# Two tiles of constants padded to whole multiples of 128 bytes in a two-block transformer kernel

## The chip, the cores and the metric

The kernel runs on one NeuronCore of a Trainium2 chip. The metric is the device time of one launch in microseconds. Three runs of the kernel before gave 2766.96, 2767.59 and 2768.25 us, so the median is 2767.59 us.

## The reference

All arithmetic is in float32, for one sequence of 512 tokens of width 1024. Two blocks follow each other. Cut to what matters:

```python
def reference(x, mem, ...):
    x = first_block(x, mem, ...)
    return second_block(x, ...)

def first_block(...):
    x = x + rms_norm(hybrid_mixer(rms_norm(x)), post)            # sparse attention beside an mLSTM
    x = x + rms_norm(memory_cross_attention(rms_norm(x), rms_norm(mem)), post)
    x = x + rms_norm(swiglu_ffn(rms_norm(x), w_gate_up, w_down), post)

def second_block(...):                                            # two layers
    # per layer: h += 0.5 ffn1(h); h += conformer_conv(h) (layer 0)
    #            or stick_breaking_attention(h) with shared keys (layer 1); h += 0.5 ffn2(h)
    return rms_norm(h, final_norm)
```

Five of the stages are SwiGLU feed-forward layers: 1024 columns to twice 2816, and 2816 back to 1024. They hold most of the multiplications.

## The kernel before

Activations lie transposed, with the features over the 128 partitions and the 512 tokens along each partition. A dense stage multiplies weight blocks of 128 by 128, which are the stationary operand (they are loaded with LDWEIGHTS, written PEld in the profile), with 256 tokens at a time of the activations, which are the moving operand of the MATMUL. Each float32 product is made of three in the type fp32r: high part of the weight times high part of the activation, low times high, and high times low. So every tile of weights and every tile of activations stands in memory twice, as a high and as a low part.

SyncE streams the weights into `w_raw`, a ring of four slots of 4,096 bytes per partition. ScalarE writes the high parts (`w_hi`), VectorE the low parts (`w_lo`, and `w_below` in the feed-forward stages). The order of the work is written out by hand in one block per engine, and semaphores hold the engines together.

- Dense stages (`unit`, line 646) multiply `w_hi` and `w_lo` with `h_hi`, `h_lo`, or with `m_*` and `o_*` in the memory and output stages. Where they are the second half of a feed-forward layer ("down"), the activations lie in `t_hl`, `a_below` and, for the last chunks, in `wx`.
- The gate and up products of the feed-forward layers (`product`, line 812) are done in pairs by a scheme with seven block products in place of eight. Sums of weight blocks are needed for it. They lie in `wx` (the sums S1 and S2 and the low part of A22), in `w_lo` and in `w_hi`. The moving operand is always in `t_hl`. In these stages `wx` holds weights and is a stationary operand, in the down stages it holds activations and is a moving one.
- `cmp_unit` (line 965) is the one place where the roles are turned: the small tile `g_hl` is stationary and 256 columns of `w_hi` or `w_lo` move past it.
- The sums over features for the norms are plain float32 products with one column of `cst` as the moving operand (lines 1406 and 1413: `cv`, then `sq`, are stationary).

The tiles are placed in the order in which they are declared (from line 215 on), each at the next multiple of 32 bytes, and tiles of different phases overlay each other. `vec` is 472 floats wide (1,888 bytes) and `cst` 1,301 floats (5,204 bytes). The built program has these starts in bytes of a partition:

| tile | start | past a multiple of 128 | behind `cst` |
|---|---|---|---|
| `w_raw`, `w_below` | 16,512 | 0 | no |
| `w_lo` | 32,896 | 0 | no |
| `w_hi` | 49,280 | 0 | no |
| `x` | 65,664 | 0 | no |
| `vec` | 82,048 | 0 | |
| `cst` | 83,936 | 96 | |
| `rB`, `sq`, `acc`, `t0`, `t1` | 89,152 and on | 64 | yes |
| `h_hi`, `h_lo` | 101,696, 118,080 | 64 | yes |
| `t_hl`, `o_hi`, `yb_x`, `qT` | 134,464 | 64 | yes |
| `m_hi`, `m_lo`, `qkv`, `u_conv`, `a_below` | 160,064 and on | 64 | yes |
| `cv`, `diag_w`, `c_acc`, `c_product` | 184,576 and on | 0 | yes |
| `toep`, `decay`, `n_p`, `g_hl` | 180,192 and on | 96, `g_hl` 32 | yes |
| `wx` | 216,384 | 64 | yes |

Slots, blocks and chunks inside the tiles are multiples of 512 bytes, so a product's operands keep the residue of their tile. `u_conv` is 17,344 bytes wide, which is 135.5 times 128. That is why the tiles behind it have another residue than the others.

The diff touches the declaration of `vec` and `cst` and the two transfers that fill them.

Of the kernel before, what the change touches and what calls it, by code (L numbers as in the profile page):

```python
# [140 lines left out]
def starts(sizes):  # L141

    found, at = {}, 0
    for name, size, *_ in sizes:
        found[name], at = at, at + size
    return found, at
# [13 lines left out]
VEC, NVEC = starts(VECTORS)  # L160
CST, NCST = starts(CONSTS)


def rounds(eng, n, peel=0):

    for i in range(min(peel, n)):
        yield i
    if n > peel:
        with eng.Fori(peel, n) as i:
            yield i  # L170


class Steps:
# [14 lines left out]
    def loop(self, n, per, peel=0):  # L188
        first = self.base + self.n
        for i in rounds(self.eng, n, peel):  # L190
            self.base, self.n = first + i * per, 0
            yield i
            assert self.n == per, (self.n, per)
        self.base, self.n = first + n * per, 0


def block_program(nc, t, out):
# [4 lines left out]
    with ctx:  # L202
        def held(stack):
            return lambda name, width, dt=f32: stack.enter_context(nc.sbuf_tensor(name, [P, width], dt))

        sb = held(ctx)

        def sem(name):
            return ctx.enter_context(nc.semaphore(name))
# [6 lines left out]
            w_raw, s_raw = held(h)("w_raw", RING * UNIT), held(h)("s_raw", RING * UNIT)  # L216
        w_below, w_lo, w_hi = sb("w_below", RING * UNIT, f32r), sb("w_lo", RING * UNIT, f32r), sb("w_hi", RING * UNIT, f32r)
        x = sb("x", KC * S)
        vec, cst = sb("vec", NVEC), sb("cst", NCST)
        rB = sb("rB", S)  # L220
        sq, acc = sb("sq", 2 * S), sb("acc", S)
        t0, t1 = sb("t0", S), sb("t1", S)
# [79 lines left out]
        vec_in, cst_in, mem_in = sem("vec_in"), sem("cst_in"), sem("mem_in")  # L302
# [136 lines left out]
        def centred(eng, c):  # L439
# [3 lines left out]
            else:  # L443
                eng.wait_ge(c_conv, c + 1)

        stage_blocks = {n: b for n, _, b in STAGES}
        def in_bank(i):
            return bank[(i + 1) % 3]
# [82 lines left out]
        def _(sp):  # L531
            def load_x(i):
                sp.dma_start(cut(x, i, 2 * S), t["x"][:, 2 * i:2 * i + 2].rearrange("p c n -> p (c n)")).then_inc(x_in[i], 16)

            load_x(0)
            sp.dma_start(vec[:], t["vectors"]).then_inc(vec_in, 16)

            def load(slot, src, q):

                u = 4 * q + slot  # L540
                if not (isinstance(q, int) and u < RING):
                    sp.wait_ge(w_lo_made, u - 3)
                width = src.shape[-1]
                sp.dma_start(w_raw[:, slot * UNIT:slot * UNIT + width], src).then_inc(raw_in[slot], 16)
# [4 lines left out]
            def stage(name, w):  # L549
                w = flat(w)  # L550
                q0 = U0[name] // RING
                for it in rounds(sp, w.shape[0] // RING):
                    for j in range(RING):
                        load(j, w[bass.ds(RING * it + j, 1)].rearrange("u p n -> (u p) n"), q0 + it)
# [24 lines left out]
            def stage_down(name, w, pairs):  # L579
                w = flat(w)  # L580
                q0 = U0[name] // RING
                g_end = PAIR0[pairs] + NPAIRS[pairs]
                for it in rounds(sp, KC // 4, peel=1):
                    for j in range(12):
                        if isinstance(it, int) and it == 0 and j < RING:
                            sp.wait_ge(pair_used, 6 * (g_end - 2 + j // 2) + 4 + j % 2)
                        k0, kn = DN_KS[j % 3]
                        src = w[bass.ds(4 * it + j // 3, 1), :, k0 * P:(k0 + kn) * P].rearrange("u p n -> (u p) n")
                        load(j % RING, src, q0 + 3 * it + j // RING)

            w_in, w_cmp, w_gates = flat(t["w_in"]), flat(t["cmp_w1"]), t["w_gates"].rearrange("p k n -> p (k n)")
            for r, (kind, n) in enumerate(IN_ORDER):
                load(r % RING, {"block": w_in, "cmp": w_cmp}[kind][n] if kind != "gates" else w_gates[:, n * 4 * P:(n + 1) * 4 * P],
                     r // RING)
                if r == 0:
                    load_x(1)
                if r == 1:
                    load_x(2)
                    load_x(3)
                if r == 2:  # L600
                    sp.dma_start(cst[:], t["consts"]).then_inc(cst_in, 16)

            stage("out", t["w_out"])
            stage("xkv", t["w_xkv"])
# [37 lines left out]
        def _(pe):  # L642
# [751 lines left out]
            def ln_sums(i):  # L1394
                m = LN_ORDER[i]
                _, at, n = PIECES[m]
                if i == 0:
                    pe.wait_ge(ln_s_made, 1)
                if m == KC:

                    pe.wait_ge(ln_parts, 2)
                    pe.wait_ge(ln_var_made, 1)

                centred(pe, m)
                for b in range(at // P, (at + n) // P):
                    last = nc.tensor.matmul(bank[7][:, b:b + 1], conv_out(m)[:, b * P - at:(b + 1) * P - at], const("one"),
                                            start=i == 0 and b == 0, stop=i >= KC - 1, skip_group_check=True)
                if i >= KC - 1:
                    last.then_inc(stat_done, 1)
                pe.wait_ge(c_sq, i + 1)  # L1410
                for b in range(at // P, (at + n) // P):
                    sq_at = (i % 2) * S + b * P - at
                    last = nc.tensor.matmul(bank[6][:, b:b + 1], sq[:, sq_at:sq_at + P], const("one"), start=i == 0 and b == 0,
                                            stop=i >= KC - 1, skip_group_check=True)
                last.then_inc(stat_done if i >= KC - 1 else c_sums, 1)
# [193 lines left out]
        def _(act):  # L1609
# [434 lines left out]
            def products(m, i0, i1):  # L2044
                c, _, width = PIECES[m]
                p = SHARES[m][0]
                for i in range(i0, i1):
                    n = PRODUCT0[m] + i
                    if i == 0:
                        act.wait_ge(c_glu, m + 1)  # L2050
                    if n >= 4:
                        act.wait_ge(c_product_used, n - 3)
                    nc.scalar.activation(cut(c_product, n % 4)[:, 0:width], conv_tap(m, p + i), ACT.Identity, scale=col("w_dw", c * TAPS + p + i),
                                         bias=col("b_dw", c) if i == 0 else const("zero")).then_inc(c_product_made, 1)
# [1358 lines left out]
```

## Time and profile before

| | |
|---|---|
| runs, median (lowest to highest) | 2767.59 us (2766.96 to 2768.25) |
| the profiled execution, its own time | 2768.85 us |
| its span, first to last instruction | 2766.9 us |
| mean granted TensorE clock | 0.991 of full speed |
| instructions | 53,376, of them 22,432 MATMUL |
| HBM traffic | 253.29 MB read, 8.42 MB written |

The profiled execution took 1.26 us more than the median of the runs, which is 0.05%. PE is TensorE at matmuls, PEld its weight loads, DVE is VectorE, ACT is ScalarE, POOL is GpSimd. A matmul's duration in the profile reaches from its first column to the end of its pipeline, and consecutive ones overlap. What it costs the engine is the distance from one start to the next. In a view by stretches of time, "(x885)" is the number of instructions that touch the stretch, so the two or three that began before it are counted too.

### The profile page before, as it was taken

Reading aid. Unit: us, or ns where it says so; the run is one execution under the profiler, and the core shown is the slowest. Engines: PE = TensorE matmul, PEld = TensorE weight load, DVE = VectorE, ACT = ScalarE, POOL = GpSimd, SP = SyncE. Lnnn points to the kernel's source line nnn. Section 1 sums busy time; section 2 is a strip of 40 time slices with the busy share of each in tenths; the row PEclk is TensorE's granted clock in tenths of the full one; section 3 lists DMA queues with packets and bytes.
Section 4 is the critical chain, followed back from the end, with each engine's and each line's share of the span. In section 5 each row is a group of like instructions: output and inputs, shape, how many; then the busy total and the mean of one; then the engine's idle time right before and its main releaser. Section 6 shows DMA issues by size and latency. Waiting matters only on the chain.

```text
span 2766.9 us, 53376 instructions
## 1 busy us (share of the span) xinstructions
PE 2709.6 (98%) x22432; PEld 2586.7 (93%) x22432; DVE 1830.9 (66%) x2650; ACT 1296.3 (47%) x2052; POOL 239.4 (9%) x212
## 2 busy tenths in 40 slices
PE   8999999999999999999999999999999999999998
PEld 8977998999999999997799999999999987999998
DVE  6786753888626888348868884338886367587743
ACT  4465524545524455246754553215554246445531
POOL 0010201000000000018710000000000000100000
PEclk9999999999999999999899999999999999999999
DMA  6320431223332233322122333342333332223332
GB/s 214 110 67 17 129 101 47 92 84 102 119 102 77 85 107 113 97 90 62 39 65 89 106 105 108 92 155 84 105 106 118 94 126 88 62 87 106 99 111 73
DMA packets 76266, 265.10 MB, mean 96 GB/s; under 512 B 8388, under 2 KB 10564, under 8 KB 75776
## 3 DMA queue, kind: packets, MB, share of 16 engines
q1 hardware_dynamic: 69408, 248.93, 29.0%
q10 hardware_dynamic: 5632, 8.39, 0.8%
q0 software_dynamic: 992, 4.42, 0.5%
q8 instruction: 176, 2.88, 0.4%
q14 instruction: 58, 0.48, 0.1%
HBM read 253.29 MB, written 8.42 MB: 95 GB/s over the span
## 4 chain that ended last, share of the span: by engine, by line
PE 89%; DVE 4%; ACT 3%; issue 2%; DMA 1%; POOL 1%; SPq 0%; DVEq 0%; POOLq 0%; ACTq 0%
PE bank L646 48%; PE bank L812 30%; PE bank L701 2%; DMA w_raw<-in_w_gu 1%; DVE bank L3013 1%; PE bank L766 1%; DVE w_lo L2268 1%; POOL c_acc L3286 1%; PE bank L1463 1%; PE bank L1542 1%; PE bank L1381 1%; PE bank L1562 1%; PE bank L990 1%; PE bank L1117 1%; PE bank L1331 0%
## 5 line engine op out<-in xcount | busy, mean ns | idle before, releaser
L2268 DVE TENSOR_TENSOR w_lo<-w_raw,w_hi 128x1024 fp32r<-128x1024 f32 (+1 forms) x296 | 358.4, 1214 | 351.3 <-ACT w_hi L1621 184.7
L812 PE MATMUL bank<-t_hl,w_hi 128*128 128x256 f32 x2752 | 534.3, 282 | 17.4 <-issue 13.9
L812 PEld LDWEIGHTS bank<-t_hl,w_hi 128*128 128x128 f32 x2752 | 443.1, 189 | 19.8 <-issue 19.3
L1621 ACT ACTIVATE w_hi<-w_raw 128x1024 fp32r<-128x1024 f32 (+1 forms) x296 | 298.3, 1024 | 236.8 <-PE bank L646 156.9
L646 PE MATMUL bank<-h_hi,w_hi 128*128 128x256 f32 x1936 | 388.4, 282 | 11.4 <-DVE w_lo L2268 11.4
L646 PE MATMUL bank<-t_hl,w_hi 128*128 128x256 f32 x2128 | 386.9, 281 | 0.0
L646 PE MATMUL bank<-h_lo,w_hi 128*128 128x256 f32 x1936 | 380.0, 278 | 0.0
L646 PE MATMUL bank<-h_hi,w_lo 128*128 128x256 f32 x1936 | 379.9, 278 | 0.0
L812 PE MATMUL bank<-t_hl,wx 128*128 128x256 f32 x1720 | 360.3, 281 | 0.0
L646 PE MATMUL bank<-t_hl,w_lo 128*128 128x256 f32 x1672 | 333.8, 281 | 0.0
L812 PE MATMUL bank<-t_hl,w_lo 128*128 128x256 f32 x1720 | 331.6, 283 | 0.0
L646 PEld LDWEIGHTS bank<-h_hi,w_hi 128*128 128x128 f32 x1936 | 294.6, 189 | 20.1 <-DVE w_lo L2268 11.0
L646 PEld LDWEIGHTS bank<-t_hl,w_hi 128*128 128x128 f32 x2128 | 309.0, 188 | 0.0
L646 PEld LDWEIGHTS bank<-h_lo,w_hi 128*128 128x128 f32 x1936 | 293.9, 189 | 0.0
L646 PEld LDWEIGHTS bank<-h_hi,w_lo 128*128 128x128 f32 x1936 | 293.7, 189 | 0.0
L812 PE MATMUL bank<-t_hl,w_below 128*128 128x256 f32 x1032 | 290.9, 282 | 0.0
L812 PEld LDWEIGHTS bank<-t_hl,wx 128*128 128x128 f32 x1720 | 287.5, 189 | 0.0
L812 PEld LDWEIGHTS bank<-t_hl,w_lo 128*128 128x128 f32 x1720 | 261.5, 192 | 0.0
L646 PEld LDWEIGHTS bank<-t_hl,w_lo 128*128 128x128 f32 x1672 | 256.5, 190 | 0.0
L3238 POOL TENSOR_TENSOR acc<-acc,sq 128x512 f32<-128x512 f32 (+1 forms) x63 | 81.5, 1294 | 1648.5 <-ACT sq L1627 1646.8
L812 PEld LDWEIGHTS bank<-t_hl,w_below 128*128 128x128 f32 x1032 | 198.8, 193 | 0.0
L646 PE MATMUL bank<-a_below,w_hi 128*128 128x256 f32 x912 | 181.7, 281 | 0.0
(394 smaller groups left out, 4619.1 us busy)
## 6 DMA issues: line engine op xcount, KB each, us to landing
w_raw<-in_w_gu SPq DMA_DIRECT2D x220, 512.0 KB, 3.6
w_raw<-in_w_dn SPq DMA_DIRECT2D x80, 512.0 KB, 3.6
w_raw<-in_w_dn SPq DMA_DIRECT2D x40, 384.0 KB, 3.2
w_raw<-in_w_pw SPq DMA_DIRECT2D x24, 512.0 KB, 3.6
w_raw<-in_w_in SPq DMA_DIRECT2D x22, 512.0 KB, 4.5
w_raw<-in_w_xkv SPq DMA_DIRECT2D x16, 512.0 KB, 3.6
w_raw<-in_w_kv SPq DMA_DIRECT2D x16, 512.0 KB, 3.6
stick_qkv<-t ACTq DMA_DIRECT2D x24, 256.0 KB, 2.0
```

The lines of the kernel that those rows point to most:

```text
L646: last = nc.tensor.matmul(dst[:, c:c + HALF], w, o[:, at + c:at + c + HALF], start=start and c == 0, stop=stop, skip_group_check=True)
L701: last = nc.tensor.matmul(dst[:, 0:HALF], w[:, at:at + P], src, start=start and i == 0 and m == 0, stop=stop and i == len(ks) - 1 and m == 2)
L766: last = nc.tensor.matmul(dst, w[:, at:at + P], half_of(o, k, half), start=half == 0 and k == 0 and m == 0, stop=k == KC - 1 and m == 2, s ...
L812: last = nc.tensor.matmul(pair_bank(s, which), w[:, i * P:(i + 1) * P], o, start=start and i == 0 and m == 0, stop=stop and i == 3 and m = ...
L990: nc.tensor.matmul(bank[2 * (s % 2) + half][:, 0:nsa_n(s)], qT[rs, c * S + qb * P:c * S + (qb + 1) * P], (kS, kW)[br - 1][rs, 0:nsa_n(s)], ...
L1117: last = nc.tensor.transpose(bank[4 + half][:, k * P:(k + 1) * P], nsa_p(s, half, S)[:, k * P:(k + 1) * P], ident)
L1381: last = nc.tensor.matmul(tap_bank(m), w, conv_tap(m, k), start=k == 0, stop=k == n - 1)
L1463: last = nc.tensor.matmul(bank[PW2_BANKS[0][j]][:, tokens(half)], w[:, at:at + P], half_of(o, k, half), start=half == 0 and k == 0 and m = ...
L1542: last = nc.tensor.matmul(z[half][:, 0:n], qT_[rs, qb * P:(qb + 1) * P], kT[rs, S - n:S], start=False, stop=True, skip_group_check=True)
L1621: nc.scalar.activation(w_hi[:, at:at + n], w_raw[:, at:at + n], ACT.Copy).then_inc(w_hi_made, 1)
L2268: V.tensor_tensor(w_lo[:, at:at + n], w_raw[:, at:at + n], w_hi[:, at:at + n].bitcast(f32), sub).then_inc(w_lo_made, 1)
L3238: G.tensor_tensor(acc[:, 0:n], acc[:, 0:n], sq[:, (c % 2) * S:(c % 2) * S + n], add).then_inc(summed, 1)
```

## The change

`vec` is declared with 480 columns in place of 472, and `cst` with 1,312 in place of 1,301. That is 32 and 44 bytes, 76 in all. `vec` then ends at a multiple of 128 bytes, `cst` begins and ends at one, and what lies behind it begins 64 bytes later than before (12 of the 76 bytes were lost before to the multiple of 32). The transfers fill the same 472 and 1,301 columns as before. Nothing else is edited: the instructions, their order, their sizes and the semaphores are the same.

```diff
+def lines(width):
+
+    return -(-width // 32) * 32
+
...
-        vec, cst = sb("vec", NVEC), sb("cst", NCST)
+        vec, cst = sb("vec", lines(NVEC)), sb("cst", lines(NCST))
...
-            sp.dma_start(vec[:], t["vectors"]).then_inc(vec_in, 16)
+            sp.dma_start(vec[:, 0:NVEC], t["vectors"]).then_inc(vec_in, 16)
...
-                    sp.dma_start(cst[:], t["consts"]).then_inc(cst_in, 16)
+                    sp.dma_start(cst[:, 0:NCST], t["consts"]).then_inc(cst_in, 16)
```

After the edit, by the same order of placing, `h_*`, `t_hl`, `o_*`, `m_*`, `a_below`, `wx`, `sq` and `acc` begin at multiples of 128 bytes. `cv`, `diag_w`, `c_acc` and `c_product` begin 64 bytes past one, `g_hl` 96 past one. The weight tiles `w_below`, `w_lo`, `w_hi` lie ahead of `vec` and do not move.

## Rows read from the trace of the kernel before

**Rows 1.** The page, part 1: busy time, share of the span, instructions

```profile
PE 2709.6 (98%) x22432; PEld 2586.7 (93%) x22432; DVE 1830.9 (66%) x2650; ACT 1296.3 (47%) x2052; POOL 239.4 (9%) x212
```

**Rows 2.** The page, part 4: the chain that ended last

```profile
PE 89%; DVE 4%; ACT 3%; issue 2%; DMA 1%; POOL 1%; SPq 0%; DVEq 0%; POOLq 0%; ACTq 0%
PE bank L646 48%; PE bank L812 30%; PE bank L701 2%; DMA w_raw<-in_w_gu 1%; DVE bank L3013 1%; PE bank L766 1%; DVE w_lo L2268 1%; POOL c_acc L3286 1%; PE bank L1463 1%; PE bank L1542 1%; PE bank L1381 1%; PE bank L1562 1%; PE bank L990 1%; PE bank L1117 1%; PE bank L1331 0%
```

**Rows 3.** Busy time by stretches, PE alone: stretch, length, busy (instructions), granted clock

```profile
936.00:981.00 45.00, 45.00 (x384) 1.00 0.32 96
1238.10:1249.10 11.00, 11.00 (x96) 1.00 0.21 71
1802.00:1902.00 100.00, 100.00 (x885) 1.00 0.43 140
2100.00:2200.00 100.00, 100.00 (x851) 1.00 0.33 98
```

**Rows 4.** Line 646: count, duration in ns least/median/most, first and last start

```profile
L646 PE MATMUL bank<-t_hl,w_hi x2128: 281/281/281, 722.8 to 2739.7; 128*128 128x256 f32 x194
L646 PE MATMUL bank<-h_hi,w_hi x1936: 276/276/683, 9.9 to 2445.5; 128*128 128x256 f32 x194
...
L646 PE MATMUL bank<-t_hl,w_lo x1672: 281/281/281, 723.0 to 2739.9; 128*128 128x256 f32 x186
...
L646 PE MATMUL bank<-a_below,w_hi x912: 281/281/281, 723.2 to 2733.1; 128*128 128x256 f32 x183
...
L646 PE MATMUL bank<-wx,w_hi x304: 281/281/281, 737.4 to 2740.2; 128*128 128x256 f32 x152
```

**Rows 5.** Line 812, the same columns

```profile
L812 PE MATMUL bank<-t_hl,w_hi x2752: 276/281/552, 560.1 to 2634.2; 128*128 128x256 f32 x197
...
L812 PE MATMUL bank<-t_hl,wx x1720: 281/281/283, 561.5 to 2634.1; 128*128 128x256 f32 x192
...
L812 PE MATMUL bank<-t_hl,w_lo x1720: 276/281/415, 561.6 to 2629.9; 128*128 128x256 f32 x192
...
L812 PE MATMUL bank<-t_hl,w_below x1032: 276/281/416, 560.2 to 2628.4; 128*128 128x256 f32 x172
```

**Rows 6.** Matmuls in order of time, a feed-forward pair: start, length, instruction

```profile
923.10 0.28 PE L812 MATMUL bank<-t_hl,w_hi 128*128 128x256 f32 x1
923.21 0.28 PE L812 MATMUL bank<-t_hl,wx 128*128 128x256 f32 x1
923.33 0.28 PE L812 MATMUL bank<-t_hl,w_lo 128*128 128x256 f32 x1
```

**Rows 7.** Matmuls in order of time, a dense unit, then `cmp_unit`

```profile
133.48 0.39 PE L646 MATMUL bank<-h_hi,w_lo 128*128 128x256 f32 x2
133.71 0.40 PE L646 MATMUL bank<-h_lo,w_hi 128*128 128x256 f32 x2
133.94 0.28 PE L965 MATMUL bank<-w_hi,g_hl 128*128 128x256 f32 x1
134.06 0.28 PE L965 MATMUL bank<-w_lo,g_hl 128*128 128x256 f32 x1
```

**Rows 8.** Lines 1406 and 1413, columns of rows 4; last, eight in order of time

```profile
L1406 PEld LDWEIGHTS bank<-cst,cv x64: 188/192/333, 1304.3 to 1378.8; 128*128 128x128 f32 x64
...
L1413 PEld LDWEIGHTS bank<-cst,sq x64: 186/192/333, 1305.5 to 1379.7; 128*128 128x128 f32 x64
L1413 PE MATMUL bank<-cst,sq x64: 250/250/352, 1305.5 to 1379.8; 128*128 128x1 f32 x64
...
1305.51 1.03 PE L1413 MATMUL bank<-cst,sq 128*128 128x1 f32 x8
```

**Rows 9.** Groups of instructions by form, ScalarE: busy us, mean ns

```profile
L1627 ACT ACTIVATE sq<-x 128x512 f32<-128x512 f32 x47 | 29.8, 634 | 305.9 <-DVE x L2486 277.6 <-DVE x L3126 28.2
L1627 ACT ACTIVATE sq<-yb_x 128x512 f32<-128x512 f32 x8 | 5.0, 622 | 3.4 <-DVE yb_x L2918 3.1 <-POOL acc L3234 0.2
```

**Rows 10.** Stretch of a feed-forward layer: PE, PEld, DVE, ACT, POOL busy, clock

```profile
590.00:850.00 260.00, 258.81 (x2194) 258.14 (x2193) 148.47 (x211) 112.54 (x172) 9.82 (x8) 1.00 0.34 105
```

## The prediction

> **What bounds the kernel now.** I read the page first. TensorE is busy for 98% of the span [rows 1], and the chain that ended last is 89% TensorE, 78% of it in the two lines that do dense products, L646 and L812 [rows 2]. So the question is what one of these matmuls costs, from its start to the next.
>
> The view by stretches answers that, at a full granted clock in each. From 1802 to 1902 us 885 matmuls touch the stretch. About 2.4 of them began before it (0.276 us long, one each 0.113 us), so the step is 100 / 882.6 = 113.3 ns. From 2100 to 2200 us it is 100 / 848.6 = 117.8 ns. The other two stretches are at the slow value: 936 to 981 us gives 117.9, 1238 to 1249 us 117.5 [rows 3]. It is one instruction on the same shapes, with **two speeds 4.5 ns apart**. The durations show them too: 276 ns and 281 ns.
>
> Which products run at which? The rows by operand are the key view. With `h_hi` moving, the median is 276. With `t_hl`, `a_below` or `wx` moving in L646 all 5,016 take 281, least and most [rows 4]. In L812 three of four kinds have a least of 276, but the 1,720 with weights in `wx` never go under 281 [rows 5].
>
> The order of time shows the switch itself. Up to 923.21 us the starts lie 0.11 us apart. With the first weights from `wx` they become 0.12 apart, and the speed stays low for all of 936 to 981 us, although most of the products there use `w_hi` and `w_lo` [rows 3, 6]. The other place is `cmp_unit`: two products in a row with `h_hi` take 0.39 us together, the last two with `h_lo`, while the first weights from `g_hl` are being loaded, take 0.40, and the step behind them is 0.12 [rows 7]. `wx` lies 64 bytes past a multiple of 128, and `g_hl` 32. All other weights of these products lie at a multiple. So my reading: the slow pace holds itself. A weight load from an address off the 128 bytes throws the engine into it, and with nothing to interrupt the stream it stays there, through the whole down stage behind as well. An interruption can also end in either pace: 1238 to 1249 us is slow with `h_hi` and no `wx` near it [rows 3].
>
> **The change, part by part.** *The two transfers.* They move the same bytes with the same number of issues, and no instruction is added or moved. Cost 0; only the place of `cst` differs, by 32 bytes.
>
> *ScalarE, VectorE, GpSimd.* Their tiles change residue. A square read from `x` (at a multiple of 128) takes 634 ns and one read from `yb_x` (64 past) 622 ns [rows 9]. The one that lies better is not faster, so I take 0. If there were a gain, it would be hidden: in a feed-forward layer VectorE is busy 148.5 of 260 us and ScalarE 112.5 [rows 10], and TensorE does not wait for them. That cover also stays if TensorE is 4% faster.
>
> *Plain float32 products.* For the convolution `cv` and `diag_w` go from 0 to 64 past, away from the multiple. With one moving column the step is set by the weight load alone: (1.03 - 0.25) / 7 = 0.1114 us for `sq`. Its load (64 past) has a median of 192 ns, and so has that of `cv` (0 past) [rows 8]. Same price, so 0. These rows also speak against a simple penalty per load: the misplacement costs only while a full-rate moving stream runs beside it.
>
> *The fp32r products.* This is the one term with a size. Weights from `wx` come to lie at a multiple of 128. L812 has 2752 + 1720 + 1720 + 1032 = 7,224 matmuls [rows 5], and the down stages in L646 have 5,016 [rows 4]. If all 12,240 went from 117.8 to 113.3 ns, that is 12,240 x 4.5 = 55 us. Not all will. Interruptions remain (the plain float32 products, waits), and after them it is open which pace comes, as 1238 to 1249 us shows. For `h_hi`, where no `wx` disturbs, the median is fast, so more than half is [rows 4]. I take 70% as an estimate between that half and all: 0.7 x 55 = 39 us. The bounds of this term: 55 us and a little more if the dense stages also lose their slow parts, and half, 27 us.
>
> *Moving operands.* They go from 64 past to 0 past. No row has an fp32r stream with both operands at 0. Bounds: at best the step falls to that of the load alone, 111.4 ns [rows 8], which is 1.9 ns on the 12,240 and on the 5,808 with `h_hi` and `h_lo` (three kinds of 1,936 [rows 4]), 34 us. At worst it is the slow speed for all. I take 0, since the quick pace exists with 64 past already.
>
> **Sum.** Against the profiled execution 2768.85 - 39 = 2730 us, and its time is 1.3 us above the median of the runs, so 2728.6 us; I say 2728. Late next is TensorE again; nothing else comes near.
>
> **The rivals.** *A: nothing changes (2767.6 us).* What `wx` and `g_hl` share besides their residue is that both lie high in the partition, at 216,384 and 209,312, while `w_hi`, `w_lo` and `w_below` lie under 65,664. If the trigger is that a weight load and a moving operand lie in the same region, 64 bytes move nothing. For it: both switches in the trace fit it as well [rows 6, 7]. Against it: at `g_hl` the moving tile is `h_lo` at 118,080, so a region would have to begin between 65,664 and 118,080, a border for which no row speaks. A change of less than 0.2% (5.5 us), about what a measurement of this kernel can tell from none, is counted here. The Trainium skill (SBUF — State Buffer, "Door 1", the note on cachelines) gives SBUF lines of 16 bytes, with a price for each crossing into a new one. Old and new starts are all multiples of 16, so by that rule no crossing is saved, and the time would stay at 2767.6 us. The trace has a switch at `wx`, which that rule does not tell apart from `w_hi`.
>
> *B: slower (up to 2793 us).* Perhaps it is not the weights' own residue that counts but how the two operands lie to each other. The quick pace is seen only with weights at 0 and the moving tile 64 past. `wx` with `t_hl` has both at 64, a distance of 0, and there it turns slow. After the change every pair lies at a distance of 0. Then the dense stages with `h_hi` and `h_lo` would lose the quick pace too. That is 5,808 x 4.5 = 26 us [rows 4], which gives 2793 us if all of them are fast now, some 2780 if half. It decides from the first dense stage on. Against it: `cmp_unit` has a distance of 32 and is slow too, so distance needs a finer rule than residue does. The Trainium skill (the same page, "Who interferes with whom") counts two independent read ports for PE, one for the moving operand and one for weight loads, and says that "PE and ACT never wait on anyone". By that rule this rival falls away, and no row here shows the ports.
>
> *C: more than forecast.* All is fast and the step falls to the load's own: 55 + 13 (half of the dense stages' 26) + 34 = 102 us, 2666 us at the very best. No row shows such a step beside a full stream, so it gets little weight.
>
> **How the numbers follow.** The forecast's case, the residue of the weights decides: 0.53, at 2700 to 2745 us. C: 0.05. A: 0.20. B: 0.22, at 2774 to 2793 us. So faster 0.58, same 0.20, slower 0.22. The range goes from 2700 us (all 55 us and the dense stages' part) over A into the lower part of B, to 2782 us. Left out are C and the upper half of B, with what the forecast's case may miss, under 0.2. The forecast's own range is 2700 to 2745 us.
>
> **What would show it.** Right: in L812 the products with `wx` have a least of 276, and the down stages of L646 a median of 276; the stretches of the feed-forward layers step at 113.3 ns at the same clock; the `h_hi` rows stay as they are; in the switch view no change of step at `wx`, but still one at `g_hl`, which goes from 32 to 96 past. A is right if rows 4 to 7 come back unchanged. B is right if the `h_hi` rows show 281 as median and 1802 to 1902 us has about 851 matmuls. The prediction is wrong in its size if the feed-forward stages are fast in some layers and slow in others to another share than 70%.

## The result and the profile after

The changed kernel takes 2832.69 us in the median of four runs (lowest 2831.63), the kernel before, measured with it, 2767.28 us. One of the four took 5367.85 us; its cause is not known, and it is left out of the ratio. The ratio is 1.0237, with a 95% interval of 1.0217 to 1.0257: 65 us slower. The forecast was 2728 us, 39 us faster.

The page of the changed kernel, first its span, then part 1 and part 4:

```profile
span 2829.7 us, 53376 instructions
...
PE 2777.7 (98%) x22432; PEld 2655.5 (94%) x22432; DVE 1832.7 (65%) x2650; ACT 1294.1 (46%) x2052; POOL 238.5 (8%) x212
...
PE 93%; DVE 3%; ACT 2%; issue 1%; DMA 0%; POOL 0%; SPq 0%; DVEq 0%; ACTq 0%; POOLq 0%
```

The count of instructions is the same. VectorE, ScalarE and GpSimd are busy for the same time within 2.2 us of [rows 1]. TensorE is busy 2777.7 - 2709.6 = 68.1 us longer, and the span has grown by 2829.7 - 2766.9 = 62.8 us. The other 5 us came back from its waits: it is idle 52.0 us in place of 57.3. So the whole loss stands in TensorE's own steps. Five lines were added at the top, so line 646 is now 651, 812 is 817 and 965 is 970.

Lines 651 and 817, least/median/most duration in ns, as in [rows 4, 5]:

```profile
L651 PE MATMUL bank<-t_hl,w_hi x2128: 283/283/283, 741.6 to 2802.6; 128*128 128x256 f32 x194
L651 PE MATMUL bank<-h_hi,w_hi x1936: 278/283/682, 10.3 to 2505.2; 128*128 128x256 f32 x194
...
L817 PE MATMUL bank<-t_hl,w_hi x2752: 278/283/554, 577.4 to 2695.1; 128*128 128x256 f32 x197
L817 PE MATMUL bank<-t_hl,wx x1720: 283/283/283, 578.8 to 2695.0; 128*128 128x256 f32 x192
```

The step by stretches, as in [rows 3]:

```profile
1850.00:1900.00 50.00, 50.00 (x419) 1.00 0.43 134
2100.00:2200.00 100.00, 100.00 (x836) 1.00 0.35 105
```

Both paces of before, 276 and 281 ns long, are gone. Nearly all products (19,375 of 20,136) are 283 ns long now. Less the 2.4 that overlap the edge, the steps are 50 / 416.6 = 120.0 ns and 100 / 833.6 = 120.0 ns, at a full granted clock. At 2.4 GHz that is 288 cycles; the quick pace of before, 113.3 ns, is 272. In order of time, a dense stage:

```profile
942.11 0.40 PE L651 MATMUL bank<-h_lo,w_hi 128*128 128x256 f32 x2
942.35 0.40 PE L651 MATMUL bank<-h_hi,w_hi 128*128 128x256 f32 x2
942.59 0.40 PE L651 MATMUL bank<-h_hi,w_lo 128*128 128x256 f32 x2
942.83 0.40 PE L651 MATMUL bank<-h_lo,w_hi 128*128 128x256 f32 x2
```

Each pair of matmuls takes 0.24 us, and hardly anything changes: between the starts of consecutive products of this kind the trace has 120 ns nearly everywhere (6,056 of 6,480 with `h_hi` or `h_lo`, 5,241 of 5,280 in the down stages). Before, it had 113 or 114 ns in 4,687 of those 6,480.

### The profile page after: what moved, and what is told of

Same layout as the page of the kernel before. It is cut to its first block, busy times and chain, and to the rows that moved or that the text cites. A ratio compares the mean times of both kernels' runs of the same rounds, so it can differ in the third digit from the quotient of the medians.

```text
span 2829.7 us, 53376 instructions
## 1 busy us (share of the span) xinstructions
PE 2777.7 (98%) x22432; PEld 2655.5 (94%) x22432; DVE 1832.7 (65%) x2650; ACT 1294.1 (46%) x2052; POOL 238.5 (8%) x212
## 4 chain that ended last, share of the span: by engine, by line
PE 93%; DVE 3%; ACT 2%; issue 1%; DMA 0%; POOL 0%; SPq 0%; DVEq 0%; ACTq 0%; POOLq 0%
PE bank L651 50%; PE bank L817 31%; PE bank L706 2%; PE bank L1386 1%; PE bank L771 1%; PE bank L1547 1%; PE bank L1468 1%; DVE bank L3018 1%; PE bank L1567 1%; PE bank L1579 1%; PE bank L995 1%; PE bank L1122 1%; PE bank L1336 0%; PE bank L1138 0%; PE bank L1172 0%
## 5 line engine op out<-in xcount | busy, mean ns | idle before, releaser
L817 PE MATMUL bank<-t_hl,w_hi 128*128 128x256 f32 x2752 | 542.8, 285 | 13.7 <-issue 13.2
L817 PEld LDWEIGHTS bank<-t_hl,w_hi 128*128 128x128 f32 x2752 | 451.4, 193 | 14.8 <-issue 14.8
L651 PE MATMUL bank<-h_hi,w_hi 128*128 128x256 f32 x1936 | 399.4, 288 | 11.4 <-DVE w_lo L2273 11.4
L651 PE MATMUL bank<-t_hl,w_hi 128*128 128x256 f32 x2128 | 391.6, 283 | 0.0
L651 PE MATMUL bank<-h_hi,w_lo 128*128 128x256 f32 x1936 | 391.0, 284 | 0.0
L651 PE MATMUL bank<-h_lo,w_hi 128*128 128x256 f32 x1936 | 390.8, 283 | 0.0
L651 PE MATMUL bank<-t_hl,w_lo 128*128 128x256 f32 x1672 | 336.9, 283 | 0.0
L817 PE MATMUL bank<-t_hl,w_lo 128*128 128x256 f32 x1720 | 336.2, 286 | 0.0
L651 PEld LDWEIGHTS bank<-h_hi,w_hi 128*128 128x128 f32 x1936 | 303.7, 192 | 20.1 <-DVE w_lo L2273 11.3
L651 PEld LDWEIGHTS bank<-t_hl,w_hi 128*128 128x128 f32 x2128 | 315.6, 192 | 0.0
L651 PEld LDWEIGHTS bank<-h_hi,w_lo 128*128 128x128 f32 x1936 | 302.9, 193 | 0.0
L651 PEld LDWEIGHTS bank<-h_lo,w_hi 128*128 128x128 f32 x1936 | 302.8, 192 | 0.0
L817 PEld LDWEIGHTS bank<-t_hl,w_lo 128*128 128x128 f32 x1720 | 266.2, 195 | 0.0
L651 PEld LDWEIGHTS bank<-t_hl,w_lo 128*128 128x128 f32 x1672 | 260.8, 192 | 0.0
```

Source lines behind the costliest of these rows:

```text
L651: last = nc.tensor.matmul(dst[:, c:c + HALF], w, o[:, at + c:at + c + HALF], start=start and c == 0, stop=stop, skip_group_check=True)
L817: last = nc.tensor.matmul(pair_bank(s, which), w[:, i * P:(i + 1) * P], o, start=start and i == 0 and m == 0, stop=stop and i == 3 and m = ...
```

## The experiments

After the trace I had two theories. **Distance**: what counts is how far the moving operand's address lies from the stationary one's, modulo 128. It was 64 for most products before and is 0 for all of them now. **Own place**: the moving operand is slow when it begins at a multiple of 128. The forecast's theory, the weights' own place, stayed as a third. Most variants below were run once, beside the kernel before on the same chip. The nine runs of the kernel before on the chip of the first experiments lie between 2764.66 and 2773.49 us, so a difference of a few us in a single run means nothing.

### Both operands moved together

`e1_swap64` puts 64 bytes ahead of all tiles of the kernel before:

```diff
+        sb("front", 16)
         with ExitStack() as h:
             w_raw, s_raw = held(h)("w_raw", RING * UNIT), held(h)("s_raw", RING * UNIT)
```

> The kernel before with 64 bytes of padding ahead of all tiles: the weight tiles lie 64 past a multiple of 128, the moving tiles and wx at a multiple. Distance theory (only the distance of the moving from the stationary operand, modulo 128, sets the pace): the distances are those of before, so the step is 113.3 or 117.8 ns in the same places and the time is 2767 us. Theory of the moving operand's own residue (a moving tile at 0 is slow): 120 ns everywhere, 2832 us. Theory of the weights' own residue, the forecast's: every weight load from w_hi, w_lo, w_below is off the 128 bytes, the dense stages lose the quick pace, 2793 us or more.

`e2_both64` is the same edit on the changed kernel.

> The changed kernel with 64 bytes of padding ahead of all tiles: weights and moving tiles all lie 64 past a multiple of 128. Distance theory: distance 0 as in the changed kernel, step 120.0 ns everywhere, 2832 us. Theory of the moving operand's own residue: the moving tiles are where they were before, so 113.3 and 117.8 ns come back and the time is about 2767 us.

Measured: 2765.59 us and 2829.18 us, beside 2769.65 us for the kernel before. The lines of products of `e1_swap64`:

```profile
L647 PE MATMUL bank<-t_hl,w_hi x2128: 281/281/281, 720.0 to 2737.0; 128*128 128x256 f32 x194
L647 PE MATMUL bank<-h_hi,w_hi x1936: 276/276/683, 10.1 to 2441.6; 128*128 128x256 f32 x194
...
L813 PE MATMUL bank<-t_hl,wx x1720: 281/281/283, 560.4 to 2631.3; 128*128 128x256 f32 x192
```

and of `e2_both64`:

```profile
L652 PE MATMUL bank<-t_hl,w_hi x2128: 283/283/284, 740.3 to 2800.2; 128*128 128x256 f32 x194
L652 PE MATMUL bank<-h_hi,w_hi x1936: 274/283/682, 9.7 to 2501.3; 128*128 128x256 f32 x194
```

In the first, all weights lie off the 128 bytes and all moving tiles on them, and the rows are those of before, 281 and 276 [rows 4, 5]. In the second, the moving tiles are at 64 as before, and it is as slow as the changed kernel. Own place falls for either operand, as far as a move by 64 bytes can show it, and distance stands.

### Only the constants' place

`g2_d0c` leaves `vec` and the start of `cst` as they were and makes `cst` wider, so that all behind lies as in the changed kernel. `g1_apart` keeps the changed kernel's constants and moves the tiles from `h_hi` on by 64 bytes. The edit of `g2_d0c`, against the kernel before, and that of `g1_apart`, against the changed one:

```diff
-        vec, cst = sb("vec", NVEC), sb("cst", NCST)
+        vec, cst = sb("vec", NVEC), sb("cst", 1320)
```

```diff
         small = sb("small", 64)
+        sb("apart", 16)
```

> The kernel before with cst 19 columns wider, vec as it was: cst stays at its old place (96 past a multiple of 128), and all behind it lies where it lies in the changed kernel. Distance theory: 2832 us, step 120.0 ns. If the place of cst has a part in the loss, the time lies between 2767 and 2832 us.

> The changed kernel with its padded vec and cst, and 64 bytes of padding behind small, ahead of h_hi. So vec, cst, rB, sq, acc, t0 and t1 stay at their new places, and only the tiles from h_hi on move, to 64 past a multiple of 128; they lie 128 bytes behind their place in the kernel before. Distance theory (period 128 or less): the products' distances are 64 again, 2767 us. If the distance counts modulo 256 or more, another value than before, such as 2793 us or more. If the padding of the constants themselves costs, 2832 us stays.

Measured: 2833.90 us and 2763.17 us. The place of the constants has no part in it, and 64 bytes more, ahead of the activations, undo the loss. In `g1_apart` the paces are dealt out in another way, though:

```profile
L652 PE MATMUL bank<-t_hl,w_hi x2128: 276/276/280, 730.6 to 2734.6; 128*128 128x256 f32 x194
L652 PE MATMUL bank<-h_hi,w_hi x1936: 276/279/685, 10.3 to 2446.6; 128*128 128x256 f32 x194
```

The down stages are quick now and the dense stages mostly slow, the reverse of [rows 4]. These tiles lie exactly 128 bytes behind their old place. The sum hardly moves, but the distance modulo 128 is not all there is. The trace also shows where the quick pace comes from: in all five feed-forward layers it sets in behind the last load from `wx`, without an interruption, and holds through the down stage.

### The products with wx

`e3_wx64` moves only the weights in `wx`, in the kernel before:

```diff
-            wx = held(ph)("wx", 6 * BLOCK, f32r)
+            wx = held(ph)("wx", 6 * BLOCK + 16, f32r)
...
-            return wx[:, (3 * s + b) * BLOCK:(3 * s + b + n) * BLOCK]
+            return wx[:, 16 + (3 * s + b) * BLOCK:16 + (3 * s + b + n) * BLOCK]
```

> The kernel before, with only the weights in wx moved by 64 bytes, so that they lie at distance 64 from t_hl like all other weights; the activations kept in wx stay 64 past. Distance theory: the products of line 812 with wx no longer throw the stream into the slow pace; with all 12,240 products of the feed-forward layers at 113.3 in place of 117.8 ns the time is 2713 us, with 70% of them 2729 us. Rival (the trigger is that wx lies high in the partition, or that its loads carry a wait): no change, 2767 us.

Measured: 2756.12 us in eight runs, ratio to the kernel before 0.9949 (0.9934 to 0.9964). Line 812, line 646 and one stretch:

```profile
L812 PE MATMUL bank<-t_hl,wx x1720: 276/281/282, 562.0 to 2615.7; 128*128 128x256 f32 x192
```

```profile
L646 PE MATMUL bank<-t_hl,w_hi x2128: 276/281/282, 720.8 to 2721.4; 128*128 128x256 f32 x194
```

```profile
2100.00:2200.00 100.00, 100.00 (x851) 1.00 0.32 97
```

The products with `wx` can be quick now, and in the whole trace there is no passage from a quick stretch to a slow one at `wx` any more, where the trace before had 19. So the place that the prediction named is real: at `wx` a load at distance 0 stood in a stream at distance 64. But the slow pace comes back from interruptions. The stretch from 2100 to 2200 us is as slow as it was (851 in [rows 3] too), and about a third of the products of the feed-forward layers are quick, not 70%. The gain is 13 us, not 39.

`g3_apart_wx` is the same edit on `g1_apart`.

> The first of these three with the weights in wx moved by 64 bytes, so that every fp32r product of lines 646 and 812 has distance 64. If the two edits add up as the distance theory has it, 2756 us, 13 us under the kernel before, as the same edit of wx gave on the kernel before; the share of the quick pace after interruptions may differ by some us between executions.

Measured: 2749.07 us in two runs, ratio 0.9927 (0.9898 to 0.9956), 7 us under the expected 2756.

```profile
L652 PE MATMUL bank<-t_hl,w_hi x2128: 276/276/276, 727.2 to 2719.0; 128*128 128x256 f32 x194
L652 PE MATMUL bank<-h_hi,w_hi x1936: 276/279/685, 10.1 to 2431.2; 128*128 128x256 f32 x194
...
L818 PE MATMUL bank<-t_hl,wx x1720: 276/276/284, 569.9 to 2617.3; 128*128 128x256 f32 x192
```

Here all products of the down stages are quick and most of the pairs are, while the products with `h_hi` and `h_lo` stay mostly slow (16% have a step of 112 to 114 ns). The quick pace that the prediction hoped for on the 12,240 products exists. It takes another edit than the one made.

It does not come from interruptions alone. At the first loads from `wx` this trace passes from slow to quick 14 times, the reverse of the kernel before:

```profile
955.36 0.40 PE L818 MATMUL bank<-t_hl,w_hi 128*128 128x256 f32 x2
955.60 0.28 PE L818 MATMUL bank<-t_hl,w_below 128*128 128x256 f32 x1
955.72 0.28 PE L818 MATMUL bank<-t_hl,w_hi 128*128 128x256 f32 x1
955.83 0.28 PE L818 MATMUL bank<-t_hl,wx 128*128 128x256 f32 x1
955.95 0.28 PE L818 MATMUL bank<-t_hl,w_lo 128*128 128x256 f32 x1
956.06 0.39 PE L818 MATMUL bank<-t_hl,wx 128*128 128x256 f32 x2
956.29 0.28 PE L818 MATMUL bank<-t_hl,w_lo 128*128 128x256 f32 x1
```

Two products take 0.24 us ahead of `wx` and 0.23 behind it. Modulo 128 all these loads have the distance 64. Modulo 256, by the starts of the tiles, `w_hi`, `w_lo` and `w_below` have 64 here and `wx` has 192. In `e3_wx64` all have 192, and its trace has no such passage.

### Other distances

`e4_d96` changes only the width of `cst`, so the products with `wx` stay at distance 0 in it. The other four also move the weights in `wx`, so that every product of lines 646 and 812 has the same distance, and three of them place tiles to 16 or 8 bytes:

```diff
-            return lambda name, width, dt=f32: stack.enter_context(nc.sbuf_tensor(name, [P, width], dt))
+            return lambda name, width, dt=f32: stack.enter_context(nc.sbuf_tensor(name, [P, width], dt, align_bytes=16))
...
-        vec, cst = sb("vec", NVEC), sb("cst", NCST)
+        vec, cst = sb("vec", NVEC), sb("cst", 1332)
...
-            return wx[:, (3 * s + b) * BLOCK:(3 * s + b + n) * BLOCK]
+            return wx[:, 20 + (3 * s + b) * BLOCK:20 + (3 * s + b + n) * BLOCK]
```

That is `f2_d48x`. The others have `cst` 1312 (`e4_d96`), 1328 (`f1_d32x`), 1308 (`f3_d80x`) or 1302 wide with 8-byte placement (`f4_d56x`), and 24, 12 and 18 in place of the 20.

> The kernel before with cst 11 columns wider (NCST of them filled): all moving tiles and wx lie 96 past a multiple of 128, the weight tiles at 0. Distance theory: a new distance with an unknown pace of its own, between 111.4 ns (the weight load alone) and 120.0 ns (distance 0); 2740 to 2832 us, and another pattern of steps than at 64. If only distance 0 is bad and all else alike: as before, 2767 us.

> All moving tiles 32 past a multiple of 128, weights at 0, the weights in wx moved by 96 bytes so that every fp32r product of lines 646 and 812 has distance 32. Distance theory: every distance has a pace of its own; at 96 the mean step was 118.3 ns, at 0 it is 120.0, at 64 it is 113.3 or 117.8. If the price only depends on how far the distance is from 64, 32 gives 118.3 ns like 96 and about 2795 us. Rival (64 is special only by its two paces, all others are at 120): 2832 us.

> Placement to 16 bytes: weight tiles 112 past a multiple of 128, moving tiles 32 past, so distance 48 for every fp32r product of lines 646 and 812, wx included. If the price falls towards 64, the step lies between those of 32 and 64; if one side of 64 has the quick pace alone, 113.3 ns throughout and about 2705 us on one of 48 and 80, and a slower one on the other.

> As the last, distance 80 (weight tiles 112 past, moving tiles 64 past). The same two outcomes: if this is the side with the quick pace alone, 113.3 ns throughout and about 2705 us, if not between 113.3 and 118.3 ns and 2740 to 2795 us. In both kernels the weights lie off the 128 bytes themselves; if their own residue mattered, both would be slow.

> Placement to 8 bytes: weight tiles 104 past, moving tiles 32 past, distance 56. If the step changes only in whole units of 16 or 32 bytes, this is like 48 or like 64 (113.3 and 117.8 ns mixed, 2750 us); if it is continuous, between the two.

The same two stretches in each: `f1_d32x`,

```profile
1850.00:1900.00 50.00, 50.00 (x431) 1.00 0.39 119
2100.00:2200.00 100.00, 100.00 (x859) 1.00 0.36 106
```

`f3_d80x`,

```profile
1850.00:1900.00 50.00, 50.00 (x427) 1.00 0.44 141
2100.00:2200.00 100.00, 100.00 (x813) 1.00 0.36 109
```

and `e4_d96`:

```profile
1850.00:1900.00 50.00, 50.00 (x425) 1.00 0.39 127
2100.00:2200.00 100.00, 100.00 (x847) 1.00 0.35 105
```

With those of the other two, worked out in the same way (count less 2.4):

| distance | step, 1850 to 1900 us (dense), ns | step, 2100 to 2200 us (feed-forward), ns | time, us |
|---|---|---|---|
| 0 (changed kernel) | 120.0 | 120.0 | 2832.69 |
| 32 | 116.7 | 116.7 | 2774.45 |
| 48 | 116.7 | 116.6 | 2772.56 |
| 56 | 118.3 | 118.4 | 2795.92 |
| 64 (before, then `e3_wx64`) | 113.3 | 117.8 | 2767.28, 2756.12 |
| 80 | 117.8 | 123.4 | 2825.42 |
| 96 | 118.3 | 118.4 | 2793.18 |

The step changes with the distance, though not to a new value each time (32 and 48 have the same mean, and so have 56 and 96), and 0 is not the only bad one: at 80 the feed-forward layers are worse still. The guesses in the expectations at how the price runs all fail. The price does not only grow away from 64 (56 is dearer than 32), neither side of 64 has the quick pace alone, and 56 is neither like 48 or 64 nor between them. Only at 64 is 113.3 ns seen over a long stretch. The kernel before took 2771.74 us beside the runs of 32, 48, 56 and 80, so the single runs of 32 and 48 (2774.45 and 2772.56) show no difference from it. In these runs the paces repeat in short patterns of a few products, such as 120, 117, 116 in the dense stretch at distance 80 and 130, 117 in its down stage. That fits two streams that meet at addresses, but no run shows the meeting itself. In the runs of 48, 56 and 80 the weights begin 112 or 104 past a multiple of 128. That only the distance counts was tested for a common move of 64 bytes, not for these places.

### One load beside 512 columns

`h1_whole` writes the dense products of 512 tokens as one matmul, in the changed kernel:

```diff
-                for c in range(0, n, HALF):
-                    last = nc.tensor.matmul(dst[:, c:c + HALF], w, o[:, at + c:at + c + HALF], start=start and c == 0,
-                                            stop=stop, skip_group_check=True)
-                return last
+                return nc.tensor.matmul(dst[:, 0:n], w, o[:, at:at + n], start=start, stop=stop, skip_group_check=True)
```

> The changed kernel (distance 0) with the dense products of 512 tokens written as one matmul of 512 columns in place of two of 256, so that a weight load stands beside 512 columns instead of 256. The distance costs because a weight load and the moving stream read beside each other, and with 256 columns the load has no slack. If that is so, the load hides behind 512 columns, and a step is 213 ns (512 columns at 2.4 GHz) plus a few, against 2 x 120 = 240 now: about 10,400 pairs of matmuls are in lines 646, 965 and 1463 with their kin, roughly 5,800 of them with h, m and o and t_hl; 20 ns off each gives 100 us, to about 2730 us. Rival: the moving stream alone is slowed at this distance, then the step is twice 120 = 240 ns and the time stays at 2832 us. The products of line 812 keep 256 columns and 120.0 ns under both.

Measured: 2755.25 us. A dense stretch, a down stretch at 2650 us, and the forms:

```profile
1830.00:1880.00 50.00, 50.00 (x222) 1.00 0.40 132
...
2650.00:2700.00 50.00, 50.00 (x222) 1.00 0.33 95
```

```profile
L814 PE MATMUL bank<-t_hl,w_hi 128*128 128x256 f32 x2752 | 540.6, 284 | 13.5 <-issue 13.2 <-ACT bank L1692 0.3
L650 PE MATMUL bank<-h_hi,w_hi 128*128 128x512 f32 x968 | 386.7, 399 | 11.9 <-DVE w_lo L2270 11.4 <-DVE h_lo L2279 0.4
```

The matmuls are 0.39 us long, so about 1.7 overlap the edge: 50 / 220.3 = 227 ns, and the trace's starts lie 226 or 227 ns apart. That is exactly twice 113.3, not the 216 I had worked out and not the rival's 240. So at distance 0 the stream of moving columns goes at the quick rate when there is one load to 512 columns, while line 814 keeps its 120 ns. What the distance makes dearer beside 256 columns is the step with a load in it. No stretch of any run has less than 113.3 ns for 256 columns (272 cycles). With 5,700 pairs at 240 - 226.7 = 13.3 ns, 76 us were to be had, and 2832.69 - 2755.25 = 77 us came.

`i1_before_whole` is the same edit on the kernel before.

> The kernel before (distance 64) with the dense products of 512 tokens as one matmul of 512 columns. If the floor is the moving stream's own, 544 cycles for 512 columns, the dense step is 226.7 ns as at distance 0, and no second pace is seen there; the products of line 812 keep their 117.8 ns. They had 120.0 in the changed kernel: 7,224 x 2.2 ns = 16 us less than its 2755 us, so about 2739 us. If a quick and a slow pace stay in the dense stages (226.7 and 235.6 ns), the slow pace is not a matter of the load's slack, and the time is 2755 us or more.

Measured: 2773.01 us, slower than at distance 0, and no faster than the kernel before (2767.98 us on that chip).

```profile
1830.00:1880.00 50.00, 50.00 (x216) 1.00 0.41 141
...
2650.00:2700.00 50.00, 50.00 (x216) 1.00 0.37 106
```

The step is 50 / 214.3 = 233 ns. So slack alone is not it: with one load per 512 columns, distance 64 costs 6.5 ns more than distance 0. My reading of the second pace as a load without slack is refuted.

`i2_best` has the wide products on `g3_apart_wx`.

> Distance 64 everywhere, wx included, the padded constants kept, and the dense products of 512 tokens as one matmul of 512 columns. If the slack theory holds: dense step 226.7 ns, line 812 at a mix of 113.3 and 117.8 ns (116.3 in the mean, as when only wx was moved), 2728 us; with line 812 quick throughout 2707 us. Rival (the slow pace comes from elsewhere and reaches the wide matmuls too): 2749 us, as without the wide matmuls.

Measured: 2732.34 us, ratio 0.9869 (0.9852 to 0.9885), near the first of the two sums. But line 815 was quicker than assumed there (114.0 ns in the mean, not 116.3) and the wide products slower (225 to 232 ns in the trace's starts, 229 in the mean, not 226.7). The two misses nearly cancel, so the time is right by luck.

### Each kind of product at its best place

`j1_split_places` puts the 64 bytes behind `h_lo` in place of ahead of `h_hi`, keeps the shift of `wx`, and uses 512 columns only with `h_hi` and `h_lo`:

```diff
         h_hi, h_lo = sb("h_hi", KC * S, f32r), sb("h_lo", KC * S, f32r)
+        sb("apart", 16)
...
+                if o is h_hi or o is h_lo:
+                    return nc.tensor.matmul(dst[:, 0:n], w, o[:, at:at + n], start=start, stop=stop, skip_group_check=True)
```

> Each kind of product at the place that was best for it so far: h_hi and h_lo at distance 0, in matmuls of 512 columns (226.7 ns there); t_hl, a_below, wx, m_* and o_* at distance 64, in matmuls of 256 columns, 128 bytes behind their old place and with the weights in wx moved by 64 bytes (mean 113.9 ns there). If the step of a product depends only on its width and on the distance of its two operands, the parts add up: against the last kernel (2732 us) the 2,904 wide products with h gain some 2.5 ns each, 7 us, and the down stages stay alike; 2725 us, and line 812 some 2 ns less on 7,224, up to 14 us more: 2711 to 2725 us. Rival (what precedes a stage decides its pace, so that the quick pace of t_hl does not stay): 2732 us or more.

Measured: 2717.58 us, inside the expected 2711 to 2725, ratio to the kernel before 0.9814 (0.9797 to 0.9830). The forms, and two stretches:

```profile
L652 PE MATMUL bank<-h_lo,w_hi 128*128 128x512 f32 x968 | 377.6, 390 | 0.0
...
L654 PE MATMUL bank<-t_hl,w_hi 128*128 128x256 f32 x2128 | 377.4, 276 | 0.0
L820 PE MATMUL bank<-t_hl,wx 128*128 128x256 f32 x1720 | 348.4, 276 | 0.0
```

```profile
1830.00:1880.00 50.00, 50.00 (x222) 1.00 0.34 111
```

The steps measured apart hold side by side: the wide products at distance 0 take 227 ns, and the products with `t_hl` have a mean duration of 276. Here too the loads from `wx` turn the slow pace into the quick one, 13 times. This version is some 50 us faster than the kernel before and 115 us faster than the changed one.

## Why the prediction was wrong

**What bounds the kernel** was right, and so was the way to see it: the step of one product, two paces 4.5 ns apart, at a full clock. The whole result lies in that step.

**The two transfers, the other engines and the plain float32 products** were put at nothing. Right: the other engines' busy times are those of before, and with `vec` and `cst` at their old starts and the rest moved (`g2_d0c`) the time is that of the changed kernel.

**The fp32r products** is the step that failed, as the prediction put it: "A weight load from an address off the 128 bytes throws the engine into it". What threw it there was a load at distance 0 from the moving operand, in a stream at distance 64. Before, `wx` with `t_hl` was the only large case of that, and it was also the only large one of weights off the 128 bytes. The two readings had the same rows. `e1_swap64` tells them apart: with all weights off the 128 bytes, every row is as before. The change did not take the bad distance from `wx`. It gave it to all others. The sum of -39 us became 12,240 x (120.0 - 117.8) = +27 us for the feed-forward layers, and for the some 7,600 other products of 256 tokens, at 114.7 ns in the mean before and 119.9 now, about +40 us. Together 67 us, where TensorE's busy time has 68.1 more.

**Moving operands** were put at 0 "since the quick pace exists with 64 past already". That sentence holds no argument for 0 past, and the same paragraph says that no row has both operands there. Its worst bound was the slow pace for all. The measured 120.0 ns lies outside it, because I took the two paces seen for the only two there are. For a relation between operands that no row shows, the rows at hand are no bound.

**Rival B** named the mechanism, the distance of the two operands, with 0.22. Its price was off. It let only the `h` products lose, by 4.5 ns, and came to 2793 us at most. In place of 117.8 there was 120.0, and the feed-forward layers had something to lose too. What I held against it, that `cmp_unit` at a distance of 32 is slow as well, was no argument: 32 is a distance with a dearer step than the quick one (116.7 ns in `f1_d32x`). `cmp_unit` itself was not tested apart.

**Rival A** and the rule on lines of 16 bytes (the Trainium skill, SBUF — State Buffer, "Door 1") gave no change. The starts at distances 0, 48, 64, 80 and 96 are all multiples of 16 apart and have five different steps, so the measurement decides against using that rule here. The same page's sentence that "PE and ACT never wait on anyone" ("Who interferes with whom"), which I had set against rival B, is of no help between PE's own two reads either: the steps of one and the same stream depend on where the weights loaded beside it lie.

The 70% too had no ground. With the same instructions, 4% of the products of the feed-forward layers have a step of 112 to 114 ns in the kernel before, 36% in `e3_wx64` and 88% in `g3_apart_wx`. In `e3_wx64` no passage of either kind stands at a load from `wx`. In `g3_apart_wx` the loads from `wx` also bring the quick pace back.

**Open.** What sets the pace after an interruption at distance 64, and whether the distance counts modulo 256 or more. For it speak the passages at `wx` in `g3_apart_wx`, that `before` and `g1_apart` differ by 128 bytes and deal the paces out in opposite ways, and that the wide products take 233 ns at the one place (`i1_before_whole`) and 225 to 232 at the other (`i2_best`). No run tells a period of 256 from a longer one. Nor is it shown why 64 is the good distance for a load beside 256 columns and 0 for one beside 512. No run shows what the memory does, so all this is a matter of steps measured at addresses.

## What to carry to other kernels

When a stream of matmuls with a weight load in each is the bound, look at the distance from start to start, over long stretches and at a known clock; if it has more than one value for the same shape, the places of its two operands against each other are worth an experiment of a few bytes of padding. Rounding everything to one boundary is not neutral: it sets all distances to 0, here the slowest kernel of the seven distances. And when two explanations share all the rows, move both operands together before trusting either.

## What was not expected of the hardware

- The step of a 256-column fp32r matmul with its weight load depends on the distance of the two operands in SBUF: 120.0 ns at 0, 116.7 at 32 and at 48, 118.3 at 56, 113.3 or 117.8 at 64, 117.8 to 123.4 at 80, 118.3 at 96.
- At distance 64 it has two paces, each of which holds for hundreds of products. In the kernel before, a load at distance 0 ended the quick one (19 times, never in `e3_wx64`, where that load is moved). In `g3_apart_wx` the loads from `wx`, at distance 64 modulo 128 but 128 bytes off the other weights modulo 256, ended the slow one 14 times.
- With 512 columns to a load the order is turned: 226.7 ns at distance 0, 233 at 64 (229 with the moving tiles 128 bytes further on).
- 113.3 ns for 256 columns, and 226.7 for 512, is the least step that a stretch of any run had.
